# A two-layer decoder trunk on one core: norm row loaded a stage ahead, logits on two column halves, gate-norm factors in the output weights

## What is computed

```python
for layer in range(2):
    x = x + mixer(rmsnorm(x, mixer_norm))
    x = x + hierarchical_moe(rmsnorm(x, moe_norm[layer]), ...)
return rmsnorm(x, final_norm)
```

```python
t = rmsnorm(x, moe_norm[layer])
g_prob = softmax(t @ w_group + b_group)                    # 4 groups, the best one is taken
e_logits = (t @ w_router + b_router).reshape(T, 4, 8)      # 2 of its 8 experts per token
```

```python
y = y * silu(z)
y = rmsnorm(y.reshape(Bsz, S, 4, 512), gate_norm.reshape(4, -1))
return y.reshape(Bsz, S, 2048) @ w_out
```

## Time and profile before

| what | value |
| --- | --- |
| runs (3): median, lowest, highest | 2836.54, 2833.12, 2842.06 us |
| profiled execution, its own time | 2830.54 us |
| its span | 2828.7 us |
| mean granted clock of TensorE | 0.97 |
| routing stages (layer 0, layer 1), from and to | 623 to 682, 2132 to 2191 us |
| expert stage of layer 0, from | 688.7 us |
| output stage of the SSD mixer, from and to | 1926.5 to 2131 us |

### The profile page before, as it was taken

The page is one execution under the profiler, slowest core; times in us unless marked ns, Lnnn a source line. Parts: engine busy times, 40 slices in busy tenths (PEclk is TensorE's granted clock), DMA queues, the critical chain, the costliest instruction groups (busy, mean ns, idle before and its releaser), DMA issues. The chain is left out here.

```text
span 2828.7 us, 40392 instructions
## 1 busy us (share of the span) xinstructions
PE 2652.8 (94%) x13859; PEld 2140.8 (76%) x13859; DVE 1882.6 (67%) x2208; ACT 1604.9 (57%) x2027; POOL 544.4 (19%) x462
## 2 busy tenths in 40 slices
PE   8998999987999999987999999998997999999992
PEld 7886667775888888876788887787884788888881
DVE  6335766535888888876572542885534888888885
ACT  4234555323888888865331233882111888888882
POOL 0000000001444444420000000440000344444440
PEclk9999999998999999998999999999998999999996
DMA  4215110024999999966242324983104899999994
GB/s 172 79 45 172 39 46 24 30 82 175 378 380 379 384 387 382 382 255 208 71 121 76 114 86 163 325 262 122 45 23 165 330 390 382 373 381 381 378 369 193
DMA packets 237958, 618.70 MB, mean 219 GB/s; under 512 B 31928, under 2 KB 76496, under 8 KB 237712
## 3 DMA queue, kind: packets, MB, share of 16 engines
q1 hardware_dynamic: 206704, 558.35, 54.6%
q0 software_dynamic: 19136, 33.61, 3.2%
q10 hardware_dynamic: 12000, 25.17, 2.6%
HBM read 566.55 MB, written 86.13 MB: 231 GB/s over the span
## 5 line engine op out<-in xcount | busy, mean ns | idle before, releaser
L2627 DVE TENSOR_TENSOR moe_w_low<-moes_raw,moe_w_high 128x2048 fp32r<-128x2048 f32 x384 | 864.9, 2286 | 146.3 <-ACT moe_w_high L2556 146.2
L2556 ACT ACTIVATE moe_w_high<-moes_raw 128x2048 fp32r<-128x2048 f32 x384 | 721.4, 1915 | 71.7 <-PEq L150 56.7
L2420 POOL COPY moe_pick<-moes_tokens 128x1 int32 (+1 forms) x64 | 107.0, 1672 | 579.6 <-PE moe_px L2469 578.5
L174 PE MATMUL moe_py<-moe_w_high,moe_h_high 128*128 128x512 f32 x512 | 209.2, 409 | 0.0
L174 PE MATMUL moe_pg<-moe_w_high,moe_x_high 128*128 128x512 f32 x512 | 204.3, 399 | 0.0
L174 PE MATMUL moe_pu<-moe_w_high,moe_x_high 128*128 128x512 f32 x512 | 204.2, 399 | 0.0
L176 PE MATMUL moe_py<-moe_w_high,moe_h_low 128*128 128x512 f32 x512 | 200.7, 392 | 0.0
L176 PE MATMUL moe_pg<-moe_w_high,moe_x_low 128*128 128x512 f32 x512 | 200.4, 391 | 0.0
L176 PE MATMUL moe_pu<-moe_w_high,moe_x_low 128*128 128x512 f32 x512 | 200.4, 391 | 0.0
L175 PE MATMUL moe_py<-moe_w_low,moe_h_high 128*128 128x512 f32 x512 | 200.1, 391 | 0.0
L175 PE MATMUL moe_pu<-moe_w_low,moe_x_high 128*128 128x512 f32 x512 | 199.6, 390 | 0.0
(11 more groups left out here) (420 smaller groups left out, 6132.4 us busy)
## 6 DMA issues: line engine op xcount, KB each, us to landing
moes_raw<-in_w_gate SPq DMA_DIRECT2D x128, 1024.0 KB, 8.2
moes_raw<-in_w_up SPq DMA_DIRECT2D x128, 1024.0 KB
moes_raw<-in_w_down SPq DMA_DIRECT2D x128, 1024.0 KB, 8.6
sproj_raw<-in_w_in_ssd SPq DMA_DIRECT2D x28, 512.0 KB, 4.3
XC<-pre SPq DMA_DIRECT2D x24, 512.0 KB, 5.1
HN<-plan_hn SPq DMA_DIRECT2D x16, 512.0 KB, 3.2
pre<-Y SPq DMA_DIRECT2D x16, 512.0 KB, 7.1
Z<-sproj_z SPq DMA_DIRECT2D x32, 256.0 KB, 2.4
```

Of the source, the lines that this page charges most:

```text
L174: nc.tensor.matmul(out, lh, rh, start=start, stop=False)
L2420: nc.gpsimd.tensor_copy(pick[a][:, :], M.tokens[:, bass.ds(b, 1)]).then_inc(picked[a], 1)
L2556: nc.scalar.activation(wh[c % SPLIT_SLOTS][:, :], M.raw[j][:, :], ACT.Copy).then_inc(w_high, 1)
L2627: nc.vector.tensor_tensor(wl[j][:, :], M.raw[c % RAW_SLOTS][:, :], bits(wh[j][:, :]), ALU.subtract).then_inc(w_low, 1)
```

## The change

A buffer `K.gain` (128 x 1024, fp32) now lives through the whole program, and three things follow.

**Norm row.** SP loads the row of layer 0's expert norm into `K.gain` at the end of `out_stage`, and that of layer 1 at the end of `ssd_out_stage`, and waits for it there. `gf` is another name for it in `plan_stage`; its load, its semaphore and DVE's wait are gone. In both projection stages the buffer stands in for weight slots that the stages had of their own (two half slots of six in `project_stage`, one of three in `ssd_project_stage`).

**Logits.** The 8 products of a pair alternate between partitions 0 to 35 and 64 to 99 of `lg`: even k sum in one, odd k in the other. `lt` has 100 partitions, its rows 32 to 63 cleared by POOL; ACT copies both halves; and turning back is a product with `fold`, a 100 x 36 matrix with two ones per column, which adds the halves.

**Gate norm.** The factors are multiplied into the output weights: ACT makes w_high with a scale of one value per partition, DVE makes w_low in one step of product and difference. The product into `whole` is gone, y_high and y_low are made from `tp` directly, and `tp` is free again only when y_low is made.

```diff
@@ project_stage
-        raw = [st.sb(f"raw{j}", [P, HALF]) for j in range(RAW)]
+        raw = [K.gain[:, j * HALF:(j + 1) * HALF] for j in range(2)] + [st.sb(f"raw{j}", [P, HALF]) for j in range(2, RAW)]
@@ out_stage, sync
                 sp.dma_start(x[t % 2][:, :], A["x"][t * P:(t + 1) * P, :]).then_inc(x_loaded[t % 2], 16)
+            sp.dma_start(K.gain[:, :], K.G[0].partition_broadcast(P)).then_inc(gain_in, 16)
+            sp.wait_ge(gain_in, 16)
@@ ssd_project_stage
-        raw = [st.sb(f"raw{j}", [P, D]) for j in range(RAW - 1)] + [K.pre[:, 4 * S + 2 * (LEFT + S):5 * S + 2 * (LEFT + S)]]
+        raw = [K.gain[:, :], st.sb("raw1", [P, D]), K.pre[:, 4 * S + 2 * (LEFT + S):5 * S + 2 * (LEFT + S)]]
@@ ssd_out_stage, sync, behind the loop over the items
+            sp.dma_start(K.gain[:, :], K.G[1].partition_broadcast(P)).then_inc(gain_in, 16)
+            sp.wait_ge(gain_in, 16)
@@ ssd_out_stage, scalar
-                    nc.scalar.activation(wh[:, k, :], w[:, k, :], ACT.Copy).then_inc(w_high, 1)
+                    g = V_GATE + half * NK + k
+                    nc.scalar.activation(wh[:, k, :], w[:, k, :], ACT.Copy, scale=K.vecs[:, g:g + 1]).then_inc(w_high, 1)
...
-                act.wait_ge(kept, n + 1)
+                act.wait_ge(turned, n + 1)
                 if n >= 2:
                     act.wait_ge(done, n - 1)
-                nc.scalar.activation(yh[n % 2][:, :, :], whole[n % 2][:, :, :], ACT.Copy).then_inc(high_ok, 1)
+                nc.scalar.activation(yh[n % 2][:, :, :], tp[n % 2][:, :, :], ACT.Copy).then_inc(high_ok, 1)
@@ ssd_out_stage, vector
-                    V.tensor_tensor(wl[:, k, :], w[:, k, :], bits(wh[:, k, :]), ALU.subtract).then_inc(w_low, 1)
+                    g = V_GATE + half * NK + k
+                    V.scalar_tensor_tensor(out=wl[:, k, :], in0=w[:, k, :], scalar=K.vecs[:, g:g + 1], in1=bits(wh[:, k, :]),
+                                           op0=ALU.mult, op1=ALU.subtract).then_inc(w_low, 1)
...
-                dve.wait_ge(turned, n + 1)
-                if n >= 2:
-                    dve.wait_ge(high_ok, n - 1)
-                    dve.wait_ge(low_ok, n - 1)
-                g = K.vecs[:, V_GATE + half * NK:V_GATE + (half + 1) * NK].unsqueeze(2).to_broadcast([P, NK, P])
-                V.tensor_tensor(whole[n % 2][:, :, :], tp[n % 2][:, :, :], g, ALU.mult).then_inc(kept, 1)
                 dve.wait_ge(high_ok, n + 1)
-                dve.wait_ge(kept, n + 1)
-                V.tensor_tensor(yl[n % 2][:, :, :], whole[n % 2][:, :, :], bits(yh[n % 2][:, :, :]), ALU.subtract).then_inc(low_ok, 1)
+                V.tensor_tensor(yl[n % 2][:, :, :], tp[n % 2][:, :, :], bits(yh[n % 2][:, :, :]), ALU.subtract).then_inc(low_ok, 1)
@@ ssd_out_stage, tensor, turn(n)
-                    pe.wait_ge(kept, n - 1)
+                    pe.wait_ge(low_ok, n - 1)
@@ plan_stage
+    HALVES = P // 2 + NL
...
-        gf = st.sb("gf", [P, D])
+        gf = K.gain
...
-        lt = st.sb("lt", [NL, S])
+        lt, fold = st.sb("lt", [HALVES, S]), st.sb("fold", [HALVES, NL])
@@ plan_stage, sync
-            sp.dma_start(gf[:, :], K.G[layer].partition_broadcast(P)).then_inc(gf_loaded, 16)
@@ plan_stage, gpsimd
+            nc.gpsimd.memset(lt[P // 4:P // 2, :], 0.0).then_inc(lt_clear, 1)
+            pool.wait_ge(lt_clear, 1)
@@ plan_stage, tensor
                 for k in range(ND):
-                    last = nc.tensor.matmul(lg[j % 2][0:NL, 0:CH], wr[:, k, :], hT[j % 2][:, k, :], start=(k == 0), stop=(k == ND - 1))
+                    first = k % 2 * P // 2
+                    last = nc.tensor.matmul(lg[j % 2][first:first + NL, 0:CH], wr[:, k, :], hT[j % 2][:, k, :], start=(k < 2), stop=(k >= ND - 2))
...
-                    last = nc.tensor.transpose(plogits[:, t, :], lt[:, t * P:(t + 1) * P], K.ident[0:NL, 0:NL])
+                    last = nc.tensor.matmul(plogits[:, t, :], lt[:, t * P:(t + 1) * P], fold[:, :], start=True, stop=True)
...
             pe.wait_ge(wr_loaded, 32)
+            pe.wait_ge(fold_ok, 1)
@@ plan_stage, scalar
                 act.wait_ge(by_expert, j + 1)
-                nc.scalar.activation(lt[:, j * CH:(j + 1) * CH], lg[j % 2][0:NL, 0:CH], ACT.Copy).then_inc(lt_ok, 1)
+                act.wait_ge(lt_clear, 1)
+                for first in (0, P // 2):
+                    last = nc.scalar.activation(lt[first:first + NL, j * CH:(j + 1) * CH], lg[j % 2][first:first + NL, 0:CH], ACT.Copy)
+                last.then_inc(lt_ok, 1)
@@ plan_stage, vector
             V.tensor_scalar(ss[:, :], K.ssq[:, :], 1.0 / D, EPS, ALU.mult, ALU.add).then_inc(mean, 1)
+            V.tensor_tensor(fold[:, :], K.ident[0:HALVES, 0:NL], K.ident[0:HALVES, P // 2:P // 2 + NL], ALU.add).then_inc(fold_ok, 1)
...
-            dve.wait_ge(gf_loaded, 16)
@@ program
+        K.gain = sb("gain", [P, D])
```

More of the change, by code:

```diff
@@ L971, in out_stage @@
         x_loaded = [st.sem(f"x_loaded{a}") for a in range(2)]
-        w_high, w_low, o_high, o_low, done, added, squares = (st.sem(n) for n in (
-            "w_high_ready", "w_low_ready", "o_high_ready", "o_low_ready", "done", "added", "squares"))
+        w_high, w_low, o_high, o_low, done, added, squares, gain_in = (st.sem(n) for n in (
+            "w_high_ready", "w_low_ready", "o_high_ready", "o_low_ready", "done", "added", "squares", "gain_in"))
         block = st.ctx.enter_context(nc.Block())
@@ L1891, in ssd_out_stage @@
         y, y_loaded, EARLY = K.y_first, K.y_loaded, 3
-        whole = [K.pre[:, a * D:(a + 1) * D].rearrange("p (k n) -> p k n", n=P) for a in range(2)]
         yh, yl = ([st.sb(f"{n}{a}", [P, NK, P], F32R) for a in range(2)] for n in ("y_high", "y_low"))
@@ L1896, in ssd_out_stage @@
         junk = st.sb("junk", [P, D])
-        mean, root, rstd_ok, scaled, turned, kept, high_ok, low_ok, w_high, w_low, done, added, squares = (st.sem(n) for n in (
-            "mean", "root", "rstd_ready", "scaled", "turned", "kept", "high_ready", "low_ready", "w_high_ready", "w_low_ready",
-            "done", "added", "squares"))
+        mean, root, rstd_ok, scaled, turned, high_ok, low_ok, w_high, w_low, done, added, squares, gain_in = (st.sem(n) for n in (
+            "mean", "root", "rstd_ready", "scaled", "turned", "high_ready", "low_ready", "w_high_ready", "w_low_ready",
+            "done", "added", "squares", "gain_in"))
         block = st.ctx.enter_context(nc.Block())
@@ L2108, in plan_stage @@
         ptab, pfirst = lg[0][:, 0:NBLK], lg[1][:, 0:NE]
-        wr_loaded, gf_loaded, mean, root, rstd_ok = (st.sem(n) for n in ("wr_loaded", "gain_loaded", "mean", "root", "rstd_ok"))
+        wr_loaded, fold_ok, lt_clear, mean, root, rstd_ok = (st.sem(n) for n in (
+            "wr_loaded", "fold_ready", "logits_cleared", "mean", "root", "rstd_ok"))
         rows, turned, kept, by_expert, lt_ok, logits = (st.sem(n) for n in (
```

## The result

| | before | changed |
| --- | --- | --- |
| first comparison: median (lowest to highest), 4 runs each | 2837.57 (2833.12 to 2842.06) us | 2812.17 (2809.95 to 2812.89) us |
| ratio, with its 95% interval | | 0.9915 [0.9901, 0.9929] |
| second comparison | 2836.36 us, 23 runs | 2815.6 us, 5 runs: 0.9926 [0.9912, 0.9940] |
| third comparison | 2836.11 us, 9 runs | 2812.45 us, 5 runs: 0.9919 [0.9906, 0.9933] |
| profiled execution, its span | 2830.54, 2828.7 us | 2812.89, 2810.8 us |

The change makes the kernel faster: the medians of the three comparisons lie 25, 21 and 24 us apart. The forecast of 20.3 us is a ratio of 0.9928, which lies inside all three intervals, close to the small end of the gain in the first one; 2816.2 us was 4 us too high, within the range.

The account below looks back on a forecast made before the run. PE was taken as the bound up to L (the end of the routing logits), DVE's chain after it. Terms -4.3 - 11.8 - 4.2 = -20.3 us took the median from 2836.5 to 2816.2 us; range 2808 to 2826.

Parts of the forecast that it names:

- Rival E: Routing stages' gains are not passed on because weights or rows arrive late; only -4.2, so 2832.3 us; chance 0.03.
- Norm row, -4.3 forecast: Start of both routing stages: DVE's waits of 1.97 and 2.37 us for the row go, -1.95 and -2.35 us.
- Logits, -11.8 forecast: Routing logits on two halves: per layer -7.1, given back +0.9 for turning back and +0.3 for the last eviction.
- The step from the attention's rows: Attention products alternating between the same halves showed a factor of 2; so a pair's logits take 1.8, not 3.58 us.
- Rival B: Logits halves do not run side by side; that term becomes +1.2 us per layer, so 2830.4 us; chance 0.07.
- rival C: Each change between whole array and halves at the logits drains it, 16 x 0.38 us, so 2822.3; chance 0.06.
- Rival D: Clock falls to 1.2 GHz from the first logits on; slower than before by 8.5 to 19.3 us, 2850; chance 0.05.
- Gate norm, -4.2 forecast: SSD output stage: first product -1.9, slow clock -1.7, other y_low waits -0.8, longer wait at second half +0.2 us.
- The first product: SSD output stage: y_low(0) is ready sooner, so PE starts at 1933.65 instead of 1935.53, -1.9 us.
- The dip of the clock: SSD output stage: with PE's gap 0.8 instead of 2.7 us, the half-rate stretch of 3.5 us goes, -1.7 us.
- The other waits for y_low: SSD output stage: PE's later waits for y_low go, as DVE has 1.2 us less per item, -0.8 us.
- the one from the profiled execution to the median: Whole kernel: the median of the runs was taken as 6.0 us above the profiled execution, 2836.5 against 2830.5 us.

Follow-up runs that it names:

- grouped: Changed kernel with each pair's logits products reordered, four even k first, then four odd k: 2821.34 us (5 runs), ratio to the kernel before 0.9951.
- few_fillers: Changed kernel with 2 filler transposes instead of 18 ahead of the SSD output stage's first product: 2813.12 us (one run).
- only_gate: Kernel before with only the gate norm moved into the SSD output weights: 2834.32 us (11 runs), ratio 0.9992.
- only_logits: Kernel before with only the logits split over two column halves: 2821.48 us (6 runs), ratio 0.9954.
- only_norm: Kernel before with only the norm row loaded a stage ahead: 2830.07 us (11 runs), ratio 0.9977.
- the kernel with all the fillers: Changed kernel with POOL's routing memsets held until DVE's first step and filler transposes in several PE gaps: 2813.2 us (5 runs), against 2812.45 without.

## Why the prediction was right, and where it was off

**What bounds.** It held that PE and DVE's path are all that counts and that the saving is passed on: the expert stage moved forward undiminished, and the norm row and the logits alone each show their gain in the runs; the gate norm alone is too small for them. Rival E falls.

**Norm row, -4.3 forecast, -4.25 in the trace.** Both waits went whole. fold was costed at 0 between the bounds 0 and 0.9: it shows 0.85 us, but behind DVE's first step and ahead of a root that comes later anyway, so 0 was right for the sum. The load ahead costs nothing on SP: the attention's output stage ends with the same work, and the routing stage starts 1.4 us behind it, in both kernels.

**Logits, -11.8 forecast, -10.9 in the trace.** The step from the attention's rows was right: 1.86 us, where 1.8 was taken; turning back came at 0.47 us for four passes against 0.24 for two, as costed; the last eviction costs 0.39, as 0.77 for two against 0.38. So 4 x 1.72 = 6.9 less 0.9 and 0.4 is 5.6 per layer, where the sum had 5.9. Rival B (no overlap) and rival C, the drain, both fall. The change from transposes to halves and back stays below 0.1 us here too: the rule of the Trainium skill, "TensorEngine Tiling (Array Packing)", Tiling Modes, that changing the mode drains the engine, costs nothing that these rows show: the steps into the logits and out of them are 0.20 and 0.31 us in both kernels. The same section says that tiles operate independently; the grouped order shows a bound to that (2.74 us for the 16 passes, against 1.86). Rival D falls: the granted clock was 1.00 in the logits.

**Gate norm, -4.2 forecast, -3.5 in the trace.** The first product: 1.9 forecast, 1.42 here and 2.1 in every other profile of the new path; here the first turn ran at the slow clock (1.97 us for 8 transposes, 1.10 in few_fillers). The dip of the clock: 1.7 forecast, 1.3 to 1.7 measured up to the first addition. The other waits for y_low: 0.8 went, as forecast, but w_low gave back 0.4, where 0.2 was costed (one w_low takes DVE 1.28 us now, 1.22 before).

The term that the sum lacked stands behind that wait for w_low, at the start of the second half. PE's timeline there and the stretch behind it (the granted clock is the third number from the end), before:

```profile
2034.90 0.47 PE L174 MATMUL sout_py<-sout_w_high,sout_y_high 128*128 128x512 f32 x1 [1.69 <-DVE sout_w_low L1971]
```
```profile
2035.00:2038.50 3.50, 3.50 (x16) 2.89 (x17) 3.50 (x4) 3.50 (x5) 0.00 (x0) 1.00 0.31 115
```

and in the changed kernel of the third comparison:

```profile
2024.40 0.47 PE L174 MATMUL sout_py<-sout_w_high,sout_y_high 128*128 128x512 f32 x1 [2.13 <-DVE sout_w_low L1976]
```
```profile
2024.40:2027.90 3.50, 3.50 (x9) 2.77 (x10) 3.50 (x4) 3.50 (x4) 0.00 (x0) 0.57 0.19 75
```

In seven of the nine profiles of the new path the clock falls there, in none of the four of the old. It costs 1.6 us: from the eighth addition to the ninth it is 15.8 us with it (15.5 in only_gate) and 14.2 without, against 14.9 before. The two that escaped are few_fillers and the profile of the result, so that -3.5 is in part luck. The wait alone does not settle it: only_logits waited 1.98 us there and kept the clock, only_gate 1.84 and lost it.

**The sum.** By the trace the three terms are -18.7 us, where -20.3 was forecast; with all other stretches the spans are 17.9 apart. The medians of the first comparison are 25.4 apart, of the others 21 and 24. The step that failed is the one from the profiled execution to the median: it took the profile's place among the runs as given. But before's profile lay 7 us under its median and the changed kernel's 0.7 above its own. A part is likely the clock: before's profile ran at full clock both in the attention's output and in the scan, which of the other twelve only that of the grouped kernel did (last section), and the two places are worth some 4 us. As the runs at the median have no trace, that is not shown, and the rest of the distance stays open. So the mechanisms were right and the terms some 2 us too large in sum, and that the medians lie 21 to 25 us apart is more than the terms explain: that 20.3 came so close is in part luck. The range had taken in such shifts, and held the result.

## What to carry to other kernels

Products with few output columns can be sent to two column halves in turn, so that two run at once: here that was worth 1.9 times, at the price of adding the halves, and it needs an order in which the halves change often (four passes in a row were as good as two, eight were not). A constant row that a stage waits for at its start costs what nothing else covers of its load, each time (here 1.97 and 2.37 us of some 3.8); loaded at the end of the stage ahead it cost nothing. And before a gap of PE is costed, look at the granted clock behind it, and then at who is late next: fillers took the dip away and gained nothing, since PE waited 2.16 us for DVE two items later. The same look is due at every other wait of PE: behind the one for w_low, in the middle of the stage, the clock fell in seven of nine profiles.

## What the runs showed of the hardware

**PE overlaps column halves across some four passes.** Runs of 2, 4 and 8 passes to a half took 1.86, 1.89 and 2.74 us for 16; on one half it was 3.58.

**A small DVE step is held by POOL's memset.** The TENSOR_SCALAR of 128 x 8 elements takes 0.93 us beside it, 0.17 without. The Trainium skill, "SBUF — State Buffer", section "SBUF: two separate sides", says that DVE and GpSimd share a pair of ports by an exclusive lock, which a DVE operation in a 2-port mode needs, and that the lock is held for the whole instruction. The first step's row agrees, for it ends with the memset that had started just ahead of it (625.53 and 625.50 us); which mode the step uses no row shows. The fold ends with it too, but stands behind the first step on DVE. Not every step is held: the reciprocal at 626.19 took 0.20 us inside the second memset (625.56 to 627.40).

**In the scan the clock is up early or late, whatever the kernel.** The first 5 us behind the scan's first product of L1738, in two executions of the changed kernel (first and second comparison):

```profile
1751.80:1756.80 5.00, 5.00 (x36) 4.04 (x35) 3.95 (x7) 5.00 (x15) 0.70 (x1) 1.00 1.05 399
```
```profile
1752.80:1757.80 5.00, 5.00 (x25) 5.00 (x25) 1.46 (x4) 3.83 (x12) 0.00 (x0) 0.50 1.05 399
```

Of 13 profiles, 6 show 1.00 there and 7 show 0.50, never anything between, and both occur for the same code. From that product to the next stage it is 166.9 to 168.3 us in five of the first kind (170.5 in the sixth, few_fillers), and 169.8 to 171.4 in the second kind. The attention's output stage differs in the same way (granted 1.00 from 534 to 538 us before, 0.71 in the changed kernel); of the profiles without fillers there three show full clock, before, only_norm and grouped. The Trainium skill, "TensorE: Matmul & The Clock Gate", Part 1, says that the chip watches TensorE's activity in windows that run on by themselves, not from the kernel's instructions; that one program shows both agrees with that. Filler transposes at the end of the SSD projection did not settle which it is: the profile of the kernel with all the fillers has 0.50, and its scan took 170.7 us against 167.3 beside it, more than the 2.5 it had gained in the attention's output. Some 3 us of the 9 between runs of the kernel before would follow from this one place; that it is the cause of the spread was not shown, as only profiled executions have a trace.
